# RWKV chunks: a half's front inside the levels of the half before it, and GpSimd's products on VectorE

## What is computed

```
def step(S, inp):
    r_t, w_t, k_t, v_t, kk_t, a_t = inp
    sa = jnp.einsum('bhvk,bhk->bhv', S, -kk_t)
    S = (S * w_t[:, :, None, :]
         + sa[..., None] * (kk_t * a_t)[:, :, None, :]
         + v_t[..., None] * k_t[:, :, None, :])
    y = jnp.einsum('bhvk,bhk->bhv', S, r_t)
```

## Time and profile before

| | us |
|---|---|
| median of three runs | 2475.47 (2472.58 to 2487.47) |
| the profiled execution, its own time | 2476.14 |
| its span | 2474.3 |
| busy: PE, DVE, ACT, POOL | 2249.0, 840.2, 582.5, 585.7 |
| the eight halves, first mask product to last G addition | 366.87 to 674.51 |

### The profile page before, as it was taken

How to read it: one execution, slowest core, us unless ns; L and a number is a source line. 1 busy time by engine, 2 the same in 40 slices (tenths; PEclk the granted TensorE clock), 3 DMA queues, 4 the chain that set the end, 5 groups by cost and what they waited for, 6 DMA issues and landing times.

```text
span 2474.3 us, 41370 instructions
## 1 busy us (share of the span) xinstructions
PE 2249.0 (91%) x17921; PEld 1472.3 (60%) x17921; DVE 840.2 (34%) x1741; ACT 582.5 (24%) x1209; POOL 585.7 (24%) x440
## 2 busy tenths in 40 slices
PE   8999998877789999999999979898899898889987
PEld 7888776666655568888887854433334444444442
DVE  4111315654566766223234542211221111111115
ACT  4111214442466654111123420000000000000002
POOL 5334333332111014332331321111111111111110
PEclk9999998999899999999999989999999999999999
DMA  5223211003110022221224269999999999999997
GB/s 202 85 102 128 77 70 44 12 29 121 43 58 32 1 89 97 79 60 35 60 60 173 89 230 428 430 429 429 429 428 428 431 428 429 429 429 429 428 430 292
DMA packets 73948, 538.38 MB, mean 218 GB/s; under 512 B 14152, under 2 KB 16456, under 8 KB 48032
## 3 DMA queue, kind: packets, MB, share of 16 engines
q1 hardware_dynamic: 58464, 507.55, 49.9%
q0 software_dynamic: 10240, 16.82, 1.8%
q10 hardware_dynamic: 5056, 11.28, 1.5%
HBM read 502.55 MB, written 43.52 MB: 221 GB/s over the span
## 4 chain that ended last, share of the span: by engine, by line
PE 42%; DMA 18%; DVE 3%; issue 1%; ACT 1%; DVEq 0%; POOLq 0%; ACTq 0%
PE banks L226 22%; DMA arena<-in_wg 17%; PE banks L231 6%; PE banks L233 6%; PE banks L232 6%; DMA arena<-in_wu 1%; PE banks L3185 1%; DVE arena L3489 0%; DVE arena L3479 0%; DVE arena L3329 0%; DVE wo_low L2106 0%; ACT arena L3291 0%; PE banks L1990 0%; PE banks L2814 0%; DMA arena<-in_wo 0%
## 5 line engine op out<-in xcount | busy, mean ns | idle before, releaser
L226 PE MATMUL banks<-arena 64*64 64x64 f32 (+10 forms) x13593 | 1369.8, 349 | 157.6 <-DMA arena<-in_wg 54.9
L226 PEld LDWEIGHTS banks<-arena 64*64 64x64 f32 (+4 forms) x13593 | 743.4, 152 | 722.6 <-issue 620.9
L236 ACT ACTIVATE arena<-banks 128x512 f32<-128x512 f32 (+5 forms) x357 | 195.1, 557 | 891.5 <-PE banks L226 532.7
L3179 POOL DMA_INDIRECT yb<-arena x64 | 65.0, 1016 | 789.1 <-DVE arena L3299 739.1
L3299 DVE TENSOR_SCALAR arena<-banks,arena 128x512 f32<-128x512 f32 x64 | 48.1, 751 | 503.7 <-PE banks L226 503.7
L231 PE MATMUL banks<-h1h,w2s 128*128 128x512 f32 x448 | 177.3, 396 | 1.7 <-DVE h1l L2013 1.7
L233 PE MATMUL banks<-h1h,w2s 128*128 128x512 f32 x448 | 174.6, 390 | 0.0
L232 PE MATMUL banks<-h1l,w2s 128*128 128x512 f32 x448 | 174.3, 389 | 0.0
L231 PE MATMUL banks<-hh,wlo 128*128 128x512 f32 x432 | 171.6, 397 | 0.0
L233 PE MATMUL banks<-hh,wlo 128*128 128x512 f32 x432 | 169.7, 393 | 0.0
L232 PE MATMUL banks<-hl,wlo 128*128 128x512 f32 x432 | 168.3, 390 | 0.0
(11 more groups left out here) (276 smaller groups left out, 2171.6 us busy)
## 6 DMA issues: line engine op xcount, KB each, us to landing
arena<-in_wg SPq DMA_DIRECT2D x64, 2048.0 KB, 32.9
arena<-in_wd SPq DMA_DIRECT2D x64, 2048.0 KB, 31.1
arena<-in_wu SPq DMA_DIRECT2D x63, 2048.0 KB, 26.6
arena<-in_w SPq DMA_DIRECT2D x55, 512.0 KB, 3.5
spill<-arena SPq DMA_DIRECT2D x27, 512.0 KB, 2.6
arena<-spill SPq DMA_DIRECT2D x27, 512.0 KB, 5.4
arena<-in_wo SPq DMA_DIRECT2D x16, 512.0 KB, 6.7
arena<-yb SPq DMA_DIRECT2D x8, 1024.0 KB, 13.2
```

Source lines behind the costliest of these rows:

```text
L226: return pe.e.matmul(o, l, r, start=start, stop=stop)
L236: return act.e.activation(o, i, ACT.Copy)
L3179: return pool.e.indirect_dma_start(yb, bass.IndirectOffsetOnAxis(ap=six[:, col:col + 1].bitcast(U32), axis=0), src[:, :], None, bounds_che ...
```

## The change

- The front of a half (score 0, score 1, AB, and what follows each on VectorE) is issued in levels 2, 3 and 4 of the half before it, between F and T: `early_half` gives the half that is ahead, `pe_front` and `dve_front` do one of its three parts. Halves 0 and 7 keep their front at their own start (`late_front`). `SC` and `TTm` get a second buffer.
- The identities and the TT mask of the front are VectorE's now, in `dve_front`.
- "turned" stands behind F of level 0, "end" behind T of level 0. ScalarE waits there for HG of the half before.
- yH and qG become YQ and HG: Y with Q, then H with G, in another order of the four corners (h, p) of the array. ScalarE copies Y and H; VectorE waits for each copy (`Y_copied`, `H_copied`), then adds Q and G.
- VectorE does the five prologue products: E6 = cum - E1, rk, b, K and D. The D product is the prologue's thirteenth step. GpSimd keeps the small scaling and the tail's addition.
- A half now yields 19 times, and 22 times with a late front. `SIDE` stays.

The diff, cut to its core:

```
     def dve_prologue(dve, i):
...
         yield
+        dve.wait_ge(s("cum"), i + 1)
...
+        dve.e.tensor_tensor(E6[:, :], Dn[i % 2][:, :], E1[:, :], ALU.subtract).then_inc(s("cum_before").sem, 1)
         yield
...
+        dve.e.tensor_tensor(E5_, rq[:, :], kq[:, :], ALU.mult).then_inc(s("rk").sem, 1)
...
+        dve.e.tensor_tensor(E2[:, :], E2[:, :], E4[:, :], ALU.mult).then_inc(s("b").sem, 1)
...
+        dve.e.tensor_tensor(Kt[i % 2][:, :], kq[:, :], E6[:, :], ALU.mult).then_inc(s("K").sem, 1)
+        yield
+        pcb = E1[:, 63:T:64].unsqueeze(2).to_broadcast([128, 16, 64])
+        dve.e.tensor_tensor(chunks16(Dn[i % 2][:, :]), C("id2", 0, 64).unsqueeze(1).to_broadcast([128, 16, 64]), pcb,
+                            ALU.mult).then_inc(s("D").sem, 1)
         yield
...
+    HALVES = [(i, hf) for i in range(NP) for hf in range(2)]
+    LAST_HALF = 2 * NP - 1
+
+    def half_buffer(i, hf):
+
+        n = 2 * i + hf
+        return 0 if n == LAST_HALF else n % 2
+
+    def early_half(i, hf):
+
+        n = 2 * i + hf + 1
+        return HALVES[n] if n < LAST_HALF else None
+
+    def late_front(i, hf):
+        return 2 * i + hf in (0, LAST_HALF)
...
+    def pe_front(pe, i, hf, part):
+        if part < 2:
+            pe_score(pe, i, hf, part)
+        else:
+            pe_AB(pe, i, hf)
...
     def pe_main(pe, i):
...
                     pe_F(pe, i, hf, lv, h)
                 yield
+                if lv == 0:
+                    pe_turned(pe, i, hf)
+                    yield
+                if lv >= 2:
+                    if ahead:
+                        pe_front(pe, *ahead, lv - 2)
+                    yield
...
                     pe_T(pe, i, hf, lv, h)
                 yield
+                if lv == 0:
+                    pe_ends(pe, i, hf)
+                    yield
...
+    def dve_front(dve, i, hf, part):
+        wait_buffer(dve, i, hf)
+        if part < 2:
             sc = con[:, CON["sc"]:CON["sc"] + 256].unsqueeze(1).unsqueeze(1).to_broadcast([128, 2, 2, 256])
+            u = ps["score", i, hf, part]
+            dve.wait_ge(u.full, u.v)
...
+            if part:
+                dve.wait_ge(u.free, u.v)
...
+                dve.e.tensor_tensor(A, A, C("id2", 0, 64).unsqueeze(1).to_broadcast([128, 8, 64]), ALU.add).then_inc(s("A_first").sem, 1)
+                dve.wait_ge(s("A_first"), 2 * i + hf + 1)
+                dve.e.tensor_tensor(TTm[:, :, 4:8, :], SC[:, :, :, 0, :], C("m1t", 0, 64).unsqueeze(1).unsqueeze(1).to_broadcast(
+                    [128, 2, 4, 64]), ALU.mult).then_inc(s("TT_first").sem, 1)
...
+            dve.e.tensor_tensor(TTm[:, :, 0:4, :], TTm[:, :, 0:4, :], C("id2", 0, 64).unsqueeze(1).unsqueeze(1).to_broadcast(
+                [128, 2, 4, 64]), ALU.add).then_inc(s("T_first").sem, 1)
...
     def dve_main(dve, i):
...
+                if lv >= 2:
+                    if ahead:
+                        dve_front(dve, *ahead, lv - 2)
+                    yield
                 evac_T(dve, dve.e.tensor_copy, i, hf, lv, 0)
```

More of the change, by code:

```diff
@@ L678, in wait_main @@
         if i >= 0:
-            for name in ("yH", "qG"):
+            for name in ("YQ", "HG"):
                 u = ps[name, i, 1]
@@ L937, in evac_T, with pe_score @@
             copy_(o[:, 0:2 * n].rearrange("p (b n) -> p b n", b=2), two(u)[:, :, 0:n]).then_inc(u.free.sem, 1)
+    CORNERS = ((0, 0), (1, 1), (0, 1), (1, 0))
+    def pe_score(pe, i, hf, g):
+        if hf == 0 and g == 0:
+            for name in ("A", "R", "B", "K"):
+                pe.wait_ge(s(name), i + 1)
+        AR_ = AR[i % 2]
+        u = ps.open(pe, ("score", i, hf, g), ring="main")
+        for jj, p in CHUNKS[4 * g:4 * g + 4]:
+            ts = tokens(hf, jj, p)
+            for kind, left in enumerate((Bt[i % 2], Kt[i % 2])):
+                for h in range(2):
+                    at = 512 * h + 256 * (jj % 2) + 128 * kind
+                    o = u.t[H64[p], at:at + 128].rearrange("p (a n) -> p a n", a=2)
+                    t = mm(pe, o, left[H64[h], ts], AR_[H64[h], :, ts], True, True)
+        t.then_inc(u.full.sem, 1)
@@ new lines, in pe_AB @@
+    def pe_AB(pe, i, hf):
+        u = ps.open(pe, ("AB", i, hf), ring="main")
+        for jj, p in CHUNKS:
+            ts = tokens(hf, jj, p)
+            for h in range(2):
+                at = 512 * h + jj * 64
+                t = mm(pe, u.t[H64[p], at:at + 64], AR[i % 2][H64[h], 0, ts], Bt[i % 2][H64[h], ts], True, True)
+        t.then_inc(u.full.sem, 1)
+    def pe_front(pe, i, hf, part):
[3 more added lines that the diff above has]
+            pe_AB(pe, i, hf)
@@ new lines, in pe_turned, with pe_ends @@
+    def pe_turned(pe, i, hf):
+        u = ps.open(pe, ("turned", i, hf), ring="main")
+        for jj in range(4):
+            js = slice((4 * hf + jj) * 128, (4 * hf + jj + 1) * 128)
+            pe.e.transpose(u.t[:, 256 * jj:256 * jj + 128], AR[i % 2][:, 0, js], ident)
+            t = pe.e.transpose(u.t[:, 256 * jj + 128:256 * jj + 256], vq[i % 2][:, js], ident)
+        t.then_inc(u.full.sem, 1)
+    def pe_ends(pe, i, hf):
+        pe.wait_ge(s("D"), i + 1)
+        u = ps.open(pe, ("end", i, hf), ring="main")
+        for kind, left in enumerate((Bt[i % 2], Kt[i % 2])):
+            for jj in range(4):
+                for h, p in CORNERS:
+                    ts = tokens(hf, jj, p)
+                    at = 512 * h + 256 * kind + 64 * jj
+                    t = mm(pe, u.t[H64[p], at:at + 64], left[H64[h], ts], Dn[i % 2][H64[h], ts], True, True)
+        t.then_inc(u.full.sem, 1)
@@ L983, in pe_main @@
+            n_half, SC, TTm = 2 * i + hf, SCs[half_buffer(i, hf)], TTs[half_buffer(i, hf)]
+            ahead = early_half(i, hf)
+            if late_front(i, hf):
+                for part in range(3):
+                    pe_front(pe, i, hf, part)
+                    yield
             for lv in range(5):
@@ L1124, in dve_main @@
             m1 = C("m1", 0, 64).unsqueeze(1).unsqueeze(1).to_broadcast([128, 2, 4, 64])
+            TTm = TTs[half_buffer(i, hf)]
             dve.e.tensor_tensor(TTm[:, :, 0:4, :], two(u)[:, :, 0:256].rearrange("p h (j n) -> p h j n", j=4), m1,
                                 ALU.mult).then_inc(u.free.sem, 1)
-            yield
-            yield
-            yield
+            dve.wait_ge(u.free, u.v)
+            dve.e.tensor_tensor(TTm[:, :, 0:4, :], TTm[:, :, 0:4, :], C("id2", 0, 64).unsqueeze(1).unsqueeze(1).to_broadcast(
+                [128, 2, 4, 64]), ALU.add).then_inc(s("T_first").sem, 1)
+    def dve_main(dve, i):
+        for hf in range(2):
+            ahead = early_half(i, hf)
+            if late_front(i, hf):
+                for part in range(3):
+                    dve_front(dve, i, hf, part)
+                    yield
             for lv in range(5):
@@ L1248, in dve_tail @@
         Y = Yi[i % 2]
-        for hf in range(2):
-            u = ps["yH", i, hf]
-            dve.wait_ge(u.free, u.v)
+        dve.wait_ge(s("Y_copied"), 2 * i + 2)
+        dve.wait_ge(s("H_copied"), 2 * i + 2)
         for c in range(1, 16):
```

231 lines of the change are left out of this document (85 added, 146 removed).

## The result

| | before | after |
|---|---|---|
| median, us | 2478.92 (2472.34 to 2487.47, 7 runs) | 2500.64 (2496.65 to 2503.85, 7 runs) |
| ratio | | 1.0092, 95% interval 1.0076 to 1.0107 |
| profiled execution, its span | 2476.14, 2474.3 | 2498.78, 2497.0 |
| the eight halves, us | 307.6 | 331.7 |
| mean granted clock | 0.959 | 0.955 |

The kernel became 22 us slower where 5 us less was forecast, and 2500.64 lies outside the range of 2445 to 2492. The halves go from 368.18 to 699.85 us: 24.1 us longer, for a span that is 22.7 longer. So all of it is in them: they begin 1.3 us later than before (368.18 for 366.87), and what stands behind them takes 1797.2 us for 1799.8.

What follows compares the result with a forecast made beforehand. It took a chain on VectorE's in-order queue through the eight halves (307.6 of 2474.3 us) as the bound. Changes per half summed to -4.7 us, so 2475.5 became 2471 us, range 2445 to 2492.

Steps and rivals of the forecast that it cites:

- the lead: G addition to masks of level 0, halves 1 to 6: 50 us in all go, 0.1 to 1.3 us of each stay.
- half 2 nearly link by link: Half 2 summed link by link from G addition to G addition: 36.6 us becomes 40.2, 3.6 us longer.
- The terms listed for links 3 to 4 and 4 to T: Half 2, masks of level 3 to the last T copy: work added between them, giving 8.8 and 4.2 us.
- 1.5 was entered for turned/end: Half 0, which keeps its front: 1.5 us for "turned" and "end", within +8.8 us for the half.
- a gain of 15 us more: If VectorE and GpSimd block each other over SBUF, removing GpSimd work saves 6 us per pair, not 2.5; trace spoke against.
- Part 3: End of each half, YQ and HG for yH and qG: counted as nothing, bounds -0.5 and +0.5 us a half.
- the other halves by the same rule: Halves other than 2 and 4, in us: 0 +8.8, 1 -5.5, 3 -4.7, 5 -6.0, 6 -5.5, 7 +1.0.
- 2.3 us "beyond slack": Half 3: the front of half 4 adds 2.3 us beyond slack, the K product 0.6; half 5 alike.
- The prediction's own test: First halves of a pair should be longer than second ones by 5 us or more; wrong if alike.
- Turned and end got +0.8: Level 0: ScalarE's two copies between T copies add 0.8 us, or 3.2 with lora products, table load and sigmoids; bounds 0, 4.
- rival (b): Halves 0 to 5: TensorE falls to its low clock, 3.5 us a half, 15 us lost, 2486 us; chance 0.18.
- Half 6: -5.5 forecast: Half 6: no front ahead and none to do; a 3.4 us TensorE wait with the attention's loads expected again; -5.5 us.

Runs made afterwards that it cites:

- a_turned_early: Changed kernel with "turned" and "end" ahead of level 0 again in halves 0 and 7; ratio 1.0087 to the kernel before, eight halves 328.5 us.
- b_products_dve: Kernel before with only the five prologue products moved to VectorE; ratio 1.0005, eight halves 307.6 us.
- a_identities_pool2: Changed kernel with identities and TT mask back on GpSimd, its small bonus scaling two steps earlier; ratio 1.0105 to the kernel before, halves 331.2 us.
- b_yq_hg: Kernel before with only YQ and HG in place of yH and qG; ratio 1.0019, eight halves 310.3 us.
- a_identities_gap: Changed kernel with early fronts' identities and TT mask behind the last T copy, still on VectorE; ratio 1.0062 to the kernel before, halves 323.5 us.
- a_silu_15: Changed kernel with the tail's silu moved from step 12 to 15 for pairs 0 and 1; ratio 1.0071 to the kernel before, halves 324.9 us.
- c_second_turned: c_second_gap_silu with "turned" and "end" ahead of level 0 in halves 0, 1, 3, 5 and 7; ratio 1.0079 to the kernel before, halves 324.7 us.
- b_turned_level0: Kernel before with "turned" and "end" in level 0 and second buffers, fronts at their own half's start; ratio 1.0164, eight halves 345.9 us.
- the c_second pair: c_second_gap_silu and c_second_turned, which differ in "turned" and "end" in five halves; ratios 1.0142 and 1.0079 to the kernel before.
- b_front_early: Kernel before with early fronts, "turned" and "end" in level 0 and two buffers; products, identities, yH and qG unchanged; ratio 1.0125, halves 337.1 us.
- a_turned_lead: Changed kernel with "turned" and "end" ahead of level 0 in all halves; ratio 1.0082 to the kernel before, eight halves 323.9 us.
- The best form with early fronts: c_gap_silu_filler: changed kernel with identities behind the last T copy, silu at step 15 and dummy TensorE products; ratio 1.0045 to the kernel before, halves 316.8 us.
- c_second_gap_silu: Changed kernel with early fronts only in halves 1, 3 and 5, identities behind the last T copy, silu at step 15; ratio 1.0142 to the kernel before.

## Why the prediction was wrong

**What held.** The place (halves only), the chain on VectorE's queue, the lead (43 us less), half 2 nearly link by link, halves 0, 2 and 4 within 1.1 us, masks of level 0 1.0 to 1.1 us behind G in halves 2 to 6 (at once in half 1), GpSimd nearly empty, level 3 the longest in halves 2 and 4 (link 3 to 4, 8.9 us; in halves 3 and 5 it was link 1 to 2, with 7.8 and 8.0). The terms listed for links 3 to 4 and 4 to T in half 2 add up to 8.9 and 4.5, where 8.8 and 4.2 were written, and that is what ran. Half 0 is partly luck: its link 0 to 1 grew by 3.4 us where 1.5 was entered for turned/end, and a_turned_early, which takes them out, leaves it at 6.8 for 7.1. A product of 1024 columns takes 1.22 us throughout:

```profile
L833 DVE TENSOR_TENSOR arena<-arena 128x1024 f32<-128x1024 f32 x3 | 3.6, 1214 | 0.0
```

The products were right at no net cost (b_products_dve). The prediction drew a gain of 15 us more from the rule of the Trainium skill (SBUF — State Buffer, Who interferes with whom); no run shows such a gain, and its own terms, 3.5 us for each of three pairs, make 10.5. The trace agrees with the rule itself: in a_identities_pool2, L810 began at 461.26 beside GpSimd's L1224, which ended at 462.47, and ended 1.08 us after it, where it takes 1.22 alone. And b_yq_hg, at +0.2%, was near the bound that I gave to Part 3 (0.5 us a half, 4 us).

**The step that failed** is "the other halves by the same rule". Half 2 was worked out gap by gap. For halves 1, 3, 5 and 6 I took the lead off nearly whole. Against it stood the front of the next half, in half 3 with 2.3 us "beyond slack", in half 5 alike, and in half 1 with no working; half 6, with no front to do, had nothing entered for its later levels. The prediction's own test said it: "I am wrong if the halves of a pair are alike". They are: 40.2 and 41.5, 38.9 and 41.0; and VectorE, forecast over 26 us busy in halves 2 to 5, is at 27.6, 23.5, 27.6 and 23.7. The miss, by links:

- Levels 2 to the last T copy in halves 3 and 5: +5.8 us each, where 2.3 + 0.6 was entered; in half 1 +7.6. The 5.2 us of a front find little slack, as a_identities_gap showed: there the 2.1 us of identities in each of six fronts, moved out of the way, gave 8 of 12.6 us back.
- Level 1 to 2 in halves 3 and 5: +3.6 and +3.8, entered at nothing. Turned and end got +0.8 for ScalarE's copies. I named the prologue's table load as a neighbour there, and not the tail's silu with two, 3.6 us on ScalarE's queue. a_silu_15 measured it: 7 us in the two halves. In this the cause is shown by a run.
- From T copy to G in half 3: +2.6, of it 2.1 for YQ/HG at the low clock; WU was at the low level before too and adds 0.3. That is rival (b), chance 0.18, in small. I had put it in halves 2 and 4, where the clock stood at 0.96. Half 3 as a whole stood at 0.84 for 0.86 before, half 5 at 0.92 for 0.92; the larger falls were in half 6 (0.77 for 0.90) and half 7 (0.88 for 0.95).
- Half 6: -5.5 forecast, +2.0 measured. Its lead fell by 5.1, its links from level 3 to the last T copy rose by 7, where the attention's steps stand at the new stops. That these steps are the cause is not shown: no run took this half apart.
- Half 7: +1.0 forecast, +4.6 measured: lead +1.8, link 0 to 1 +4.4. Turned and end are at most a part that the runs don't settle: a_turned_early took 0.9 us off, c_second_turned 3.2 against its partner. The rope operations that now stand in its front are argued from the timeline.

**What the sum never asked.** It took the front as 8.2 us that a half gets rid of. The front held the products and identities, and under the identities, for nothing, "turned", "end", and four stops of tail and prologue. The runs split the change so: "turned" and "end" to level 0, with the stops +38 us (b_turned_level0; of it some 22 are theirs by an estimate from the c_second pair, 14.2 us over five halves carried to eight, though half 0 there went the other way), the fronts of six halves to the half before -9 (b_front_early) and the rest -5. Against a kernel with "turned" and "end" already in level 0 the early front is a gain (it also has 19 stops for 22 there, which no run holds equal); against the kernel before no run shows one. It pays for a cover that it takes away itself. With turned and end back in the lead (a_turned_lead) that cover is gone, and with the front back (c_second_turned) the lead is. The best form with early fronts loses 0.45%.

**What stays open**: how the 38 us divide between "turned"/"end" and the four stops (`SIDE` was not adapted in any run), how much of the early front's 9 to 11 us is stops, halves 6 and 7, and whether another split of prologue steps over the longer half would turn the early front into a net gain.

## What to carry to other kernels

A stretch that looks like pure latency may be the cover of work on other engines: before shortening it, list all that every engine does in it, and give each item its new cover, in time and in TensorE's clock. Work moved into the gaps of a chain costs by its place in the in-order queue: it belongs behind the instruction that releases the next link, and on each engine one must look at what now stands ahead of that instruction, table loads included. When halves or stages differ, work out each of them gap by gap; carrying one's sum to the others was nearly the whole error here.

## What was new of the hardware

- TensorE's clock stood at 0.50 through 4 us with 0.32 us of work and the 4 full ones behind them (c_second_gap_silu), and the same eight transposes took 0.42 us each for 0.27, WU 3.67 for 1.96. With the transposes and "end" beside the wait, the clock stayed at 1.00 behind it (c_second_turned).
- A silu of 1024 columns with a table load on either side takes 3.6 us of ScalarE's queue: 1.28 for each load, 1.06 for itself.
- VectorE's T identity took 1.69 us for 0.69 beside GpSimd's product of 1024 columns (2.35 us) in half 3, so one product left on GpSimd is enough to stretch VectorE. That product itself took 2.35 us in all four of its places, beside VectorE's work or not.
